# An output product run in chunks inside the last attention turn

## The reference

```
fox_out  = fox(q, k, v, c) * silu(fg)           # 8 heads of 64: softmax with forget sums
pool_out = multiscale_pool(px) * silu(pg)       # 256 wide
sb_out   = stick_breaking(sq, sk, sv) * silu(sg)# 4 heads of 64
mixed = concatenate([fox_out, pool_out, sb_out])
out = x + einsum('bse,ed->bsd', mixed, w_out)   # 1024 x 1024 x 1024
```

## Time and profile before

| | us |
|---|---|
| median of 3 runs | 2799.48 (2799.42 to 2804.69) |
| the profiled execution, its own time | 2797.17 |
| its span, first to last instruction | 2795.4 |
| last stick-breaking turn, i = 41 on | about 2601 to 2684 |
| output stage, up to the last add | 2684 to 2790 |

### The profile page before, as it was taken

How to read it: one execution, slowest core, us unless ns; L and a number is a source line. 1 busy time by engine, 2 the same in 40 slices (tenths; PEclk the granted TensorE clock), 3 DMA queues, 4 the chain that set the end, 5 groups by cost and what they waited for, 6 DMA issues and landing times. The chain is left out here.

```text
span 2795.4 us, 46640 instructions
## 1 busy us (share of the span) xinstructions
PE 2332.8 (83%) x18720; PEld 1880.0 (67%) x18720; DVE 1442.4 (52%) x1831; ACT 803.4 (29%) x1215; POOL 558.8 (20%) x231
## 2 busy tenths in 40 slices
PE   8596767964899959599999995979859999999769
PEld 6464545754899927478888884858647777777447
DVE  1447777638667352456666664020454555645541
ACT  2223333101233331422233323121333433433220
POOL 0323443200000042222222221423132111110011
PEclk9798888986999979799999997999979999999879
DMA  6134433555666450011111224242112111100042
GB/s 228 38 106 132 133 121 95 169 148 135 157 158 166 94 230 30 16 60 68 68 68 68 81 83 151 103 145 83 60 46 76 31 46 46 41 29 16 8 166 83
DMA packets 253627, 264.15 MB, mean 94 GB/s; under 512 B 172568, under 2 KB 208024, under 8 KB 245536
## 3 DMA queue, kind: packets, MB, share of 16 engines
q1 hardware_dynamic: 248864, 245.12, 27.6%
q10 hardware_dynamic: 4608, 16.78, 1.9%
HBM read 196.81 MB, written 65.04 MB: 94 GB/s over the span
## 5 line engine op out<-in xcount | busy, mean ns | idle before, releaser
L105 PE MATMUL e_ps<-h_hi,e_w_hi 128*128 128x512 f32 x704 | 276.0, 392 | 32.1 <-POOL e_w_lo L1850 32.1
L1874 DVE SCALAR_TENSOR_TENSOR e_acc<-e_grid,vec,e_acc 128x1024 f32<-128x1024 f32 x176 | 264.4, 1502 | 42.6 <-DVE e_acc L1874 37.3
L105 PE MATMUL e_ps<-h_lo,e_w_hi 128*128 128x512 f32 x704 | 274.7, 390 | 0.0
L105 PE MATMUL e_ps<-h_hi,e_w_lo 128*128 128x512 f32 x704 | 274.6, 390 | 0.0
L105 PE MATMUL b_ps<-h_hi,b_w_hi 128*128 128x512 f32 (+1 forms) x488 | 195.6, 401 | 42.5 <-POOL b_w_lo L639 35.0
L1850 POOL TENSOR_TENSOR e_w_lo<-raw_up,e_w_hi 128x1024 fp32r<-128x1024 f32 x44 | 116.2, 2643 | 370.8 <-ACT e_w_hi L1821 370.8
L105 PE MATMUL g_ps<-h_hi,g_w_hi 128*128 128x512 f32 x392 | 160.1, 408 | 35.0 <-POOL g_w_lo L2363 35.0
L105 PE MATMUL b_ps<-h_lo,b_w_hi 128*128 128x512 f32 (+1 forms) x488 | 188.6, 386 | 0.0
L105 PE MATMUL b_ps<-h_hi,b_w_lo 128*128 128x512 f32 (+1 forms) x488 | 188.1, 385 | 0.0
L1978 PE MATMUL f_ps<-f_z_hi,f_w_hi 128*128 128x512 f32 x352 | 142.0, 403 | 48.5 <-DVE f_z_lo L2026 39.9
L105 PEld LDWEIGHTS e_ps<-h_hi,e_w_hi 128*128 128x128 f32 x704 | 132.7, 188 | 65.6 <-issue 38.4
(11 more groups left out here) (325 smaller groups left out, 5153.2 us busy)
## 6 DMA issues: line engine op xcount, KB each, us to landing
raw_up<-w_ffn SPq DMA_DIRECT2D x22, 1024.0 KB, 5.0
raw_down<-w_down SPq DMA_DIRECT2D x16, 1408.0 KB, 6.2
c_op<-ops SPq DMA_DIRECT2D x40, 512.0 KB, 4.5
b_adaw<-ada_rows ACTq DMA_DIRECT2D x32, 512.0 KB, 3.6
ops<-b_ops SPq DMA_DIRECT2D x16, 1024.0 KB, 4.9
raw<-w SPq DMA_DIRECT2D x29, 512.0 KB, 3.7
raw_in<-w SPq DMA_DIRECT2D x26, 512.0 KB, 6.9
zs<-e_z SPq DMA_DIRECT2D x22, 512.0 KB, 2.6
```

What stands on the lines that cost most here:

```text
L105: last = nc.tensor.matmul(out, w[:, k, :], x[:, k, cols], start=(k == 0 and n == 0), stop=(k == nk - 1 and n == 2))
L1874: a = nc.vector.scalar_tensor_tensor(out=acc[:], in0=view, scalar=wt, in1=acc[:], op0=ALU.mult, op1=ALU.add)
```

## The change

`output` is gone. Its eight weight tiles (o0 to o7) follow the projection tiles in the same weight queue, and a ninth, oz, holds the rows of the last mix tile for all eight outputs. Each finished `out` is split by ACT (`split_out`) and POOL (`out_low`) into two float32r tiles, both stored. When the last projection is done, SP loads the first six mix tiles (two parts each) over h_hi and h_lo, the normed input, and later the seventh. The product over seven mix tiles is 16 parts (`out_part`, 21 matmuls, all through bank ps[1]), placed at p = 3 to 7 of the last turn and after it, each added by DVE (`add_part`) to the x3 tile in `acc`. The last mix tile is split in place by halves (`split_m3`, `m3_low`), and its 16 products of 3 matmuls (`out_final`, four banks) come last, each with an add and a store of half a tile. `sc` moves from `rstd` to `logits`. The diff, cut to its core:

```diff
+    OUT0 = len(TILES)
+    TILES += [f"o{j}" for j in range(KD)] + ["oz"]
...
+    MIX = [4, 5] + list(range(FOX)) + [6 + n for n in range(SB)]
+    PARTS = 2 * KD
+    SLOTS_OF = {3: 2, 4: 2, 5: 3, 6: 3, 7: 3, 8: 3}
+    slot_at = lambda p: sum(SLOTS_OF.get(x, 0) for x in range(p))
+    SPLIT_AT = {4: [OUT0 + 2], 5: [OUT0 + 3], 6: [OUT0 + 4], 7: [OUT0 + 6]}
+    SPLIT_AFTER = {6: OUT0 + 5, 7: OUT0 + 7}
...
+        out, out_hi, out_lo = sb("out", [P, SEQ]), sb("out_hi", [P, SEQ], F32R), sb("out_lo", [P, SEQ], F32R)
+        own = sb("own", [P, 3, SEQ])
...
-        sc, px = rstd, pt[:].rearrange("p x b c -> p x (b c)")
+        sc, px = logits, pt[:].rearrange("p x b c -> p x (b c)")
...
+        m_hi, m_lo = h_hi, h_lo
+        acc = [own[:, 0], own[:, 1], own[:, 2], sq[:, 0], sq[:, 1], rstd[:, 0], rstd[:, 1], v[:]]
+        final_bank = [pb[b][:, cols(g)] for b in range(2) for g in range(2)]
...
+            def store(o):
+                sp.wait_ge(sem("out_hi"), o + 1)
+                sp.dma_start(d["mix2"][0, :, MIX[o]], out_hi[:].bitcast(F32)).then_inc(sem("stored"), 16)
+                sp.wait_ge(sem("out_lo"), o + 1)
+                sp.dma_start(d["mix2"][1, :, MIX[o]], out_lo[:].bitcast(F32)).then_inc(sem("stored"), 16)
+
+            def load_mixed(o, done):
+                sp.dma_start(m_hi[:, MIX[o]].bitcast(F32), d["mix2"][0, :, MIX[o]]).then_inc(done, 16)
+                sp.dma_start(m_lo[:, MIX[o]].bitcast(F32), d["mix2"][1, :, MIX[o]]).then_inc(done, 16)
...
-            for w in range(9, 12):
+            store(0)
+            for w in range(9, 11):
                 load(w)
-            for n in range(TURNS):
-                for w in range(12 + 4 * n, min(NW, 16 + 4 * n)):
+            store(1)
+            load(11)
...
+                if n == LAST - 1:
+                    for j in range(3):
+                        load_x3(j)
+                    sp.wait_ge(sem("chunk"), chunk[(f"g{LAST}", 1)] + 1)
+                    sp.wait_ge(sem("stored"), 32 * (2 + n))
+                    for o in range(2 + n):
+                        load_mixed(o, sem("mixed"))
+                store(2 + n)
+            sp.wait_ge(sem("stored"), 32 * (2 + LAST))
+            load_mixed(1 + LAST, sem("mixed_last"))
+            load(OUT0 + 3)
+            sp.wait_ge(sem("silu"), 2 + 2 * TURNS)
+            sp.wait_ge(sem("normed"), 4 * FOX)
+            sp.wait_ge(sem("chunk"), len(CHUNKS))
+            for j in range(3, KD):
+                load_x3(j)
+                if j % 2:
+                    load(OUT0 + 4 + (j - 3) // 2)
+            for w in range(OUT0 + 7, OUT0 + KD + 1):
+                load(w)
+            for f in range(PARTS):
+                g, j = f // KD, f % KD
+                sp.wait_ge(sem("added"), PARTS + f + 1)
+                sp.dma_start(d["out"][j][:, cols(g)], acc[j][:, cols(g)]).then_inc(sem("finished"), 16)
+            sp.wait_ge(sem("finished"), 16 * PARTS)
...
+            def out_part(c):
+
+                j, g = c // 2, c % 2
+                w = OUT0 + j
+                if g == 0:
+                    pe.wait_ge(sem("lo"), w + 1)
+                if c == 0:
+                    pe.wait_ge(sem("read"), len(CHUNKS))
+                    pe.wait_ge(sem("mixed"), 32 * (1 + LAST))
+                else:
+                    pe.wait_ge(sem("added"), c)
+                for a, k in enumerate(MIX[:2 + LAST]):
+                    if c == 0 and a == 1 + LAST:
+                        pe.wait_ge(sem("mixed_last"), 32)
+                    for b, (ww, x) in enumerate(((w_hi, m_hi), (w_hi, m_lo), (w_lo, m_hi))):
+                        mm = nc.tensor.matmul(ps[1][:], ww[:, w % 2, k], x[:, k, cols(g)], start=(a == 0 and b == 0),
+                                              stop=(a == 1 + LAST and b == 2))
+                mm.then_inc(sem("part"), 1)
+
+            def out_final(f):
...
+                s, k = (OUT0 + KD) % 2, MIX[2 + LAST]
+                if f == 0:
+                    pe.wait_ge(sem("lo"), OUT0 + KD + 1)
+                    for h in range(2):
+                        pe.wait_ge(sem(f"weights{h}"), PAIRS_ALL)
+                if j == 0:
+                    pe.wait_ge(sem("m3_lo"), g + 1)
+                    pe.wait_ge(sem("added"), PARTS + f - 3)
+                for b, (ww, x) in enumerate(((w_hi, m_hi), (w_hi, m_lo), (w_lo, m_hi))):
+                    mm = nc.tensor.matmul(final_bank[f % 4], ww[:, s, j], x[:, k, cols(g)], start=(b == 0), stop=(b == 2))
+                mm.then_inc(sem("final"), 1)
...
+            for i in range(PAIRS_ALL):
+                slots = SLOTS_OF.get(p, 0) if n == LAST else 0
+                scores(i)
+                if n < LAST:
                     project_dense(n + 1, p)
+                if slots:
+                    out_part(slot_at(p))
                 if i:
                     values(i - 1)
-                if i < PAIRS_ALL:
-                    turn_weights(i, 0)
-                if more:
+                turn_weights(i, 0)
+                if n < LAST:
                     project_after(n + 1, p)
-                if i < PAIRS_ALL:
-                    turn_weights(i, 1)
+                if slots:
+                    out_part(slot_at(p) + 1)
+                turn_weights(i, 1)
+                if slots > 2:
+                    out_part(slot_at(p) + 2)
+            out_part(PARTS - 3)
+            values(PAIRS_ALL - 1)
+            out_part(PARTS - 2)
+            out_part(PARTS - 1)
+            for f in range(PARTS):
+                out_final(f)
...
+            def split_out(o):
+
+                act.wait_ge(sem("out"), o + 1)
+                if o:
+                    act.wait_ge(sem("stored"), 32 * o)
+                A(out_hi[:], out[:], ACT.Copy).then_inc(sem("out_hi"), 1)
+
+            def split_m3(g):
+                act.wait_ge(sem("gated"), LAST * QT + 4 * (g + 1))
+                A(m_hi[:, MIX[2 + LAST], cols(g)], out[:, cols(g)], ACT.Copy).then_inc(sem("m3_hi"), 1)
...
+                if p == 5:
+                    split_out(0)
+            split_out(1)
             for i in range(PAIRS_ALL):
                 n, p = i // QT, i % QT
+                if n == LAST:
+                    for w in SPLIT_AT.get(p, ()):
+                        split_hi(w)
+                    if p == 5:
+                        act.wait_ge(sem("chunk"), len(CHUNKS))
+                        split_m3(0)
                 for h in range(2):
                     (weights if n < FOX else betas)(i, h)
-                if n + 1 < TURNS:
+                if n < LAST:
                     project(n + 1, p)
+                elif p in SPLIT_AFTER:
+                    split_hi(SPLIT_AFTER[p])
+            split_m3(1)
+            split_hi(OUT0 + KD)
 
...
+            def out_low(o):
+                pool.wait_ge(sem("out_hi"), o + 1)
+                if o:
+                    pool.wait_ge(sem("stored"), 32 * o)
+                nc.gpsimd.tensor_tensor(out_lo[:], out[:], out_hi[:].bitcast(F32), ALU.subtract).then_inc(sem("out_lo"), 1)
+
+            def m3_low(g):
+                k = MIX[2 + LAST]
+                pool.wait_ge(sem("m3_hi"), g + 1)
+                nc.gpsimd.tensor_tensor(m_lo[:, k, cols(g)], out[:, cols(g)], m_hi[:, k, cols(g)].bitcast(F32),
+                                        ALU.subtract).then_inc(sem("m3_lo"), 1)
...
+                    if m == 0 and p == 5:
+                        out_low(0)
+                    if m and p == 1:
+                        out_low(m)
                     project(m, p)
+            out_low(TURNS)
+            for p in range(4, QT):
+                for w in SPLIT_AT[p]:
+                    split_lo(w)
+                if p == 5:
+                    m3_low(0)
+                if p in SPLIT_AFTER:
+                    split_lo(SPLIT_AFTER[p])
+            m3_low(1)
+            split_lo(OUT0 + KD)
 
...
+            def add_part(c):
+                j, g = c // 2, c % 2
+                if g == 0:
+                    dve.wait_ge(sem(f"x3_{j}"), 16)
+                dve.wait_ge(sem("part"), c + 1)
+                TT(acc[j][:, cols(g)], ps[1][:], acc[j][:, cols(g)], ALU.add).then_inc(sem("added"), 1)
+
+            def add_final(f):
+                g, j = f // KD, f % KD
+                dve.wait_ge(sem("added"), 2 * j + g + 1)
+                dve.wait_ge(sem("final"), f + 1)
+                TT(acc[j][:, cols(g)], final_bank[f % 4], acc[j][:, cols(g)], ALU.add).then_inc(sem("added"), 1)
 
...
                     dve.wait_ge(sem("spread"), i + 1)
...
+                slots = SLOTS_OF.get(p, 0) if n == LAST else 0
+                if slots:
+                    add_part(slot_at(p))
                 if i:
                     gated(i - 1)
-                if n + 1 < TURNS:
+                if n < LAST:
                     project_gate(n + 1, p)
-                unturned(i)
+                unturned(i, 0)
+                if slots:
+                    add_part(slot_at(p) + 1)
```

(73 more changed lines are left out.)

140 lines of the change are left out of this document (23 added, 117 removed).

## The result

| | before | after |
|---|---|---|
| median in the first series (4 runs each), us | 2800.37 (2799.42 to 2804.69) | 2775.39 (2774.04 to 2779.89) |
| ratio, 95% interval | | 0.9909 (0.9890 to 0.9929) |
| profiled execution, own time / span | 2797.17 / 2795.4 | 2774.04 / 2772.3 |

The output product does run inside the last turn and the kernel is 25 us faster, not 38: 14 us slower than the 2761 I named, and 0.6 us inside the upper end of the range. The page's busy row answers the earlier trace rows; the stretches answer: the end of turn 4, the start of the last turn (two rows), then the blocks of p = 4, 6 and 7, the parts and finals behind them, and all of it from the first sigmoid of p = 3 on.

The account below looks back on a forecast made before the run. It took the last turn as bound by the ACT and DVE chain, the output stage by PE alone. Terms -47.4 + 4.7 + 0.1 + 4.3 = -38.3 us gave 2761 against the median 2799.5, range 2749 to 2776.

Parts of the forecast that it names:

- the overlap: Last turn: output product runs in PE's room beside the ACT and DVE chain; last add 47.4 us earlier.
- (a): p = 0 of turns 1 to 4: ACT's output split delays its dense read, 1.2 us each, 4.7 us in all.
- (b): POOL's new subtractions slow DVE in the last turn: 1.9 us at p = 1, 2.4 at p = 6, together 4.3.
- 2754 to 2768: Whole kernel: the main case's range in us around the predicted 2761, chance 0.55.
- reload late: Rival, part 0: mix tiles land late, part 0 loses up to 10 us, total 2771; 2768 to 2778, chance 0.10.
- clock falls: Rival, between last-turn parts: PE's waits lower its clock, with longer handshakes +6 to +10 us; 2767 to 2778, chance 0.15.
- slow start: Part 0 at p = 3 of the last turn: 12 of 21 matmuls at 0.43 us, 7.1 us in all.
- The last turn: From p = 3 scores on, worked through in PE's order: last add ends at 2742.6 instead of 2790.0, 47.4 us less.
- the multiply: p = 6 of the last turn: the split of o5 falls on the second head's `left`, costing 2.4 us.
- The other splits fall on adds and copies out of PSUM: POOL's remaining new subtractions meet only DVE adds and copies out of PSUM, priced at 0.
- clock low throughout: Rival, whole last turn: single bank keeps PE's clock at its lower level, about 2839 us; chance 0.03.
- no overlap: Rival: a misread wait makes the parts run in series with the last turn, 2796 us; 2785 to 2797, chance 0.04.

Follow-up runs that it names:

- e5: Changed kernel with ACT's output split behind its dense read, p = 7 weight splits behind the reads, DVE's first add between the heads: 2740.76 us, ratio 0.9790.
- e8: Changed kernel with only turn 4's weight split at p = 7 (o1) moved behind that group's reads: 2768.50 us, ratio 0.9882.
- e2: Changed kernel with ACT's weight split at p = 7 of every turn moved behind its read of the transposed values: 2752.80 us, ratio 0.9811.
- e4: Kernel before, with its weight split at p = 7 moved behind the read of the transposed values: 2792.55 us, ratio 0.9967.
- e1: Changed kernel with ACT's split of the finished tile at p = 0 moved behind its read of the dense product: 2767.01 us, ratio 0.9861.
- e3: Changed kernel with DVE's first part add of each last-turn block between the two heads, not behind both: 2766.38 us, ratio 0.9857.
- e7: Changed kernel with all 16 parts, their adds and the splits they need moved behind the last turn: 2823.82 us, ratio 1.0091.

## Why the prediction came out as it did

The mechanism and the signs were right: the overlap, and the terms (a) and (b). Of 38.3 us forecast, 30.2 came in this stretch; the start of the program, by chance, took 7.5 of them in the profiled pair. The 2775.39 lies outside the 2754 to 2768 that I gave 0.55 and among the times of two rivals, of which one is false (reload late) and the other true in another place (clock falls). The miss of 8.1 us in the stretch is what the working had wrong; the rest is mostly the start, which went against the change in this series (the second gave 2768.94). The costs up to p = 3 were 10.2 us above the forecast, and 2.1 of them were made good by a slow start that did not come.

- **The last turn.** Forecast from p = 3 on: 47.4 less, with 2.4 given back by the multiply, 45.0. Measured 47.1. The slow start of part 0 that I had put in (some 2.4 us) wasn't there. PE ran the scores of p = 3 at the lower clock, and the clock rose just as part 0 began (its first matmul is at 2643.19; columns as in the stretches above):

```profile
2640.30:2643.20 2.90, 2.90 (x10) 1.39 (x9) 0.56 (x1) 0.05 (x1) 0.00 (x0) 0.50 0.08 33
2643.60:2648.20 4.60, 4.60 (x21) 3.55 (x19) 3.74 (x4) 1.61 (x4) 0.00 (x0) 1.00 0.01 4
```

That was luck: in e5 and e8 the clock rose only some 3 us into part 0, and the first sigmoids of p = 3 and 4 are 14.8 us apart. In after the first sigmoids of p = 3 to 7 came 13.5, 14.2, 21.5 and 24.0 us apart. The working has the ends of the scores 15.5, 14.2, 20.7 and 21.8 apart; the first holds part 0's slow start, and the last becomes 24.2 with the 2.4 of the multiply. The multiply of p = 6 took 3.05 us instead of 1.09: 1.96 for 2.4.
- **(a) Output split ahead of the read.** 4.7 forecast, 4.4 measured between e2 and e4. It is the loss of after's turns 1 and 2 (1.1, 1.0), and e1 removes it there.
- **The step that failed: "The other splits fall on adds and copies out of PSUM", priced 0, and no term for clock falls in the turns.** My list of overlaps counted the new subtractions one by one against adds and copies in the last turn. It skipped the split of o1, at p = 7 of turn 4, where the old weight queue had ended, and the silu that stands there ahead of the copies that PE waits for: 4.9 us to p = 1 of the last turn where I had 0.1. With that split late, e8 has 2.9 us back by p = 3. And I gave the turns no clock term, though PE stood idle 2.5 us at the end of turns 0 to 3 in the kernel before: 10.4 us were lost by the end of turn 4 for 4.7. Why the clock fell at the ends of turns 2 and 3 after and not before stays open; every changed kernel with the early weight splits (after, e1, e3, e7, e8) shows falls there (0.74 or 0.87). Up to p = 3 that is 16.9 for 6.7, and the 2.1 that the last turn did better leaves the 8.1 us that are missing. With late weight splits (e2, e4) the turns show neither, and there the change is worth 49.2 us (e5), 7 to 8 of them by e3's edit (7.7 in e3 alone).
- **(b) at p = 1.** 1.9 forecast; the scan took 1.7 longer.
- **Clock between parts.** I gave 0.15 to clock falls in the last turn. They didn't come in after and did in e1, e2 and e8, whose last turns from p = 3 on took 5.0, 4.2 and 2.7 us more (1.3 of e8's at p = 3). The rival was real, but in after its place was the turns, where I had not looked. The Trainium skill, TensorE: Matmul & The Clock Gate, "A second HAM failure mode: psum-queue depth-cycling", has a kernel whose PE idles briefly between groups swing between both levels; the pairs of lines above agree for waits of 2.52 and 3.32 us, and show that the same wait need not do it.
- **Reload late, clock low throughout, no overlap.** None of them came. The six tiles' 12 DMAs were issued from 2612.86 to 2618.24, the seventh's reload at 2633.77, and part 0 began at 2643.19 without a wait. e7 shows what no overlap is: 48 us more, and 18 slower than before. "No overlap" was priced at 2796, some 4 us faster than before: it took the parts in series without the hand-overs of the bank.
- **Splits beside DVE, the rule.** The Trainium skill, SBUF — State Buffer, "Who interferes with whom", has DVE and GpSimd take turns at one port pair when the DVE operation has two SBUF inputs. Silu (0.68 to between 2.5 and 2.9 us), scan (0.69 to 2.38) and multiply (1.09 to 3.05) all agree, and adds from PSUM at 0.69 did too. I priced it rightly and didn't look for every place at which it applies.
